# Second layer's attention run in steps between the eighths of the key, value and output products

## The reference, cut to what matters

```
kv = rms_norm(h, kv_norm_g) @ w_kv_b              # 1024 -> 2048
k1, k2, vb = split(kv)                            # 8 heads: 64, 64 and 128 wide
k1, k2 = rms_norm(k1, kn_b), rms_norm(k2, kn_b)
q1, q2 = rms_norm(split(rms_norm(h, ln_attn_g[1]) @ w_q), gq)
attn_map(q, k) = softmax(where(mask, q k^T * scale + bias))
a = attn_map(q1, k1) - lam * attn_map(q2, k2)
o = rms_norm(a @ vb, sub_g) * (1 - lam_init)
h = h + o @ w_o                                   # 1024 -> 1024
h = h + conv_ffn(rms_norm(h, ln_ffn_g[1]), ...)
```

## Time and profile before

| | us |
| --- | --- |
| median of three runs | 2471.53 |
| profiled execution, its own time | 2467.94 |
| its span, first to last instruction | 2466.6 |
| TensorE busy | 2309.0 (94%) |
| VectorE busy | 1464.0 (59%) |
| ScalarE busy | 933.3 (38%) |
| GpSimd busy | 454.1 (18%) |
| second layer's keys and values, 1676.6 to 1786.3 | 109.7 |
| its queries, to 1841.5 | 55.2 |
| its attention, 1847.1 to 2034.3 | 187.2 |
| its way out, to 2083.0 | 48.7 |

### The profile page before, as it was taken

How to read it: one execution, slowest core, us unless ns; L and a number is a source line. 1 busy time by engine, 2 the same in 40 slices (tenths; PEclk the granted TensorE clock), 3 DMA queues, 4 the chain that set the end, 5 groups by cost and what they waited for, 6 DMA issues and landing times.

```text
span 2466.6 us, 44116 instructions
## 1 busy us (share of the span) xinstructions
PE 2309.0 (94%) x19314; PEld 1995.0 (81%) x19314; DVE 1464.0 (59%) x2414; ACT 933.3 (38%) x1530; POOL 454.1 (18%) x245
## 2 busy tenths in 40 slices
PE   4998999999969999996999999999999999999999
PEld 1777777777757788774699999999986669999987
DVE  3678888888775533567637677333335544677632
ACT  1324443344332525233634344223345543444421
POOL 0344433433302435222220000000000002000000
PEclk7999999999989999897999999999995559999999
DMA  6531011111134234110022332333220002333332
GB/s 243 118 104 44 11 41 44 45 50 52 49 108 144 87 120 130 52 43 18 1 77 86 91 91 85 97 94 107 83 69 1 1 1 78 95 86 95 90 94 73
DMA packets 55680, 184.71 MB, mean 75 GB/s; under 512 B 6688, under 2 KB 6688, under 8 KB 55488
## 3 DMA queue, kind: packets, MB, share of 16 engines
q1 hardware_dynamic: 55488, 181.89, 24.2%
HBM read 174.99 MB, written 6.88 MB: 74 GB/s over the span
## 4 chain that ended last, share of the span: by engine, by line
PE 78%; DVE 13%; ACT 5%; issue 2%; DMA 1%; POOL 0%; SPq 0%; DVEq 0%; POOLq 0%; ACTq 0%
PE PS L518 60%; PE PS L648 4%; PE PS L981 3%; DVE ca L1695 3%; PE PS L949 3%; PE PS L964 1%; PE PS L843 1%; PE PS L904 1%; DVE Swk L2048 1%; DVE kx L1763 1%; DVE mx L2044 1%; ACT acc L1091 1%; ACT La L1091 1%; DVE Bf L1769 1%; PE PS L1062 1%
## 5 line engine op out<-in xcount | busy, mean ns | idle before, releaser
L2288 POOL TENSOR_TENSOR wlo<-raw,whi 128x1024 fp32r<-128x1024 f32 x122 | 301.3, 2471 | 979.8 <-ACT whi L1091 974.5
L518 PE MATMUL PS<-nhi,whi 128*128 128x264 f32 x2064 | 434.3, 292 | 2.4 <-DVE nlo L1936 2.4
L518 PE MATMUL PS<-nlo,whi 128*128 128x264 f32 x2064 | 422.7, 287 | 0.0
L518 PE MATMUL PS<-nhi,wlo 128*128 128x264 f32 x2064 | 420.6, 285 | 0.4 <-POOL wlo L2288 0.4
L1091 ACT ACTIVATE whi<-raw 128x1024 fp32r<-128x1024 f32 (+1 forms) x290 | 300.6, 1037 | 237.1 <-PE PS L518 209.0
L518 PEld LDWEIGHTS PS<-nhi,whi 128*128 128x128 f32 x2064 | 323.7, 191 | 18.0 <-issue 14.9
L518 PEld LDWEIGHTS PS<-nhi,wlo 128*128 128x128 f32 x2064 | 324.1, 191 | 0.6 <-POOL wlo L2288 0.6
L518 PEld LDWEIGHTS PS<-nlo,whi 128*128 128x128 f32 x2064 | 324.3, 190 | 0.0
L1607 DVE TENSOR_TENSOR wlo<-raw,whi 128x1024 fp32r<-128x1024 f32 (+1 forms) x168 | 201.2, 1198 | 187.5 <-ACT whi L1091 187.3
L518 PE MATMUL PS<-hhi,whi 128*128 128x512 f32 x648 | 264.2, 408 | 7.6 <-DVE hlo L1674 7.6
L518 PE MATMUL PS<-hhi,wlo 128*128 128x512 f32 x648 | 258.4, 399 | 1.5 <-POOL wlo L2288 1.5
(11 more groups left out here) (349 smaller groups left out, 3673.8 us busy)
## 6 DMA issues: line engine op xcount, KB each, us to landing
raw<-in_wall SPq DMA_DIRECT2D x298, 512.0 KB, 3.6
raw<-in_wall SPq DMA_DIRECT2D x16, 384.0 KB, 3.0
TZ<-g_rows SPq DMA_DIRECT2D x2, 2112.0 KB, 8.3
g_rows<-gsb SPq DMA_DIRECT2D x8, 328.0 KB
xt<-in_xT SPq DMA_DIRECT2D x1, 2048.0 KB, 13.1
o_rows<-os SPq DMA_DIRECT2D x8, 256.0 KB, 2.1
keep<-o_rows SPq DMA_DIRECT2D x8, 256.0 KB, 4.1
x<-in_xT SPq DMA_DIRECT2D x1, 2048.0 KB, 9.0
```

The lines of the kernel that those rows point to most:

```text
L518: q = e.matmul(out, cuts[a][:, k * P:(k + 1) * P], (hi_, lo_)[b][:, kr, lo:lo + w], start=start and k == 0 and a == b == 0, stop=stop and ...
L2288: e.tensor_tensor(wlo[slot[i]][:, w], raw[i % NRAW][:, w], whi[slot[i]][:, w].bitcast(F32), ALU.subtract).then_inc(*up("lo_pool", i))
```

## The change

The queries' units come first, with the rows scaled by ln_attn_g; then the operands are scaled anew by kv_norm_g. The key and value units are ordered by pairs of heads: key tiles p and 4 + p, value tiles 2p and 2p + 1. The way out is cut into 8 units of four blocks for heads 0 to 3 and 8 for heads 4 to 7, each added to H (steps res_b1 and res_b). Every program writes two lists of steps: "a" is one of four parts of an attention step, "g" one eighth of a product. A table sets their order on all engines: 32 g first (the first pair's keys and values), then for each of 8 heads the string BESIDE with 20 a and 16 g, then AFTER, whose g find nothing left. The g of heads 0 to 5 are the keys and values of the next pairs, those of heads 6 and 7 the first half of the way out.

The products keep banks 0 to 3. The attention has four: scores in 4 and 5 (one each, both for a 528 wide step), turned weights in 6, output and the turned remainder in 7. Both maps' maxima are negated in one instruction, both sums inverted in one, and ScalarE's exponentials wait for that one negation. Norms of keys use the product's own bank pair, as do the turned values; the head norm has a buffer of its own (sqb).

```diff
+BESIDE = "agagagagg" "agagagag" "agagagag" "aagaag" "aaaag"
+AFTER = "ag" * 10
...
-            for j in range(16):
-                units.append(("b_kv", j * P, 0, 8))
             for j in (0, 4, 1, 5, 2, 6, 3, 7):
                 units.append(("b_q", j * P, 0, 8))
-            for j in range(8):
-                units.append(("b_out", j * P, 0, 8))
+            for p in range(4):
+                for j in (p, 4 + p, 8 + 2 * p, 9 + 2 * p):
+                    units.append(("b_kv", j * P, 0, 8))
+            for k0 in (0, 4):
+                for j in range(8):
+                    units.append(("b_out", j * P, k0, 4))
...
+        def run_beside(attend, made):
+            for name in "g" * 32 + 8 * BESIDE + AFTER:
+                next(attend if name == "a" else made, None)
+            for part in (attend, made):
+                for _ in part:
+                    pass
...
-                    kr = order[k] if order else k0 + k
+                    kr = order[k0 + k] if order else k0 + k
...
-                normed("b_kv", ("kb_raw", k), (lambda k: on.wait_ge(*at("ffn0_n", k))) if k == 0 else None)
+                    normed("b_q", ("qb_raw", kt), (lambda k: on.wait_ge(*at("ffn0_n", k))) if (h, kt) == (0, 0) else None)
...
+            def made_beside():
+                def steps_of(what, b, hi_, lo_, rhs=None, order=None):
+                    for k, _ in enumerate(product(what, hi_, lo_, halves(T, b), rhs, order=order)):
+                        if k == 3 or (k == 1 and what == "b_out"):
+                            flush()
+                        yield
+                for p in range(4):
+                    for k in (p, 4 + p):
+                        b = banks["kb", k] = pair_of_banks(("kb_log", k))
+                        yield from steps_of("b_kv", b, nhi, nlo, (lambda k: on.wait_ge(*at("n2", k))) if k == 0 else None)
+                        def norm_k(k=k, b=b):
+                            on.wait_ge(*at("kb_sq", k))
+                            sums(sqh, T, b, blk).then_inc(*up("kb_sum", k))
+                        later.append(norm_k)
+                        yield
+                    for k in (2 * p, 2 * p + 1):
+                        b = banks["vb", k] = pair_of_banks(("Vb", k))
+                        yield from steps_of("b_kv", b, nhi, nlo)
+                        def turn_vb(k=k, b=b):
+                            on.wait_ge(*at("vb", k))
+                            turn_v(vTb[:, k % 2, :], b).then_inc(*up("vb_turned", k))
+                        later.append(turn_vb)
+                        yield
+                for j in range(8):
+                    b = pair_of_banks(("res_b1", j))
+                    yield from steps_of("b_out", b, ohi_b, olo_b, (lambda k: on.wait_ge(*at("ob", k))) if j == 0 else None, place)
+                    yield
...
+                def scores_free(bb, *then):
+                    for b in bb:
+                        for step in free_s[b]:
+                            on.wait_ge(*at(*step))
+                        free_s[b] = then
+                def scores(n, s):
+                    h, i = steps[n]
+                    q0, nq, w = rows_of(i)
+                    rows, kt = rowsof[h % 2], 4 * s + h // 2
+                    if n % 5 == 0:
+                        on.wait_ge(*at("qb", kt))
+                        on.wait_ge(*at("kb", kt))
+                    scores_free((4, 5) if w > 512 else (4 + s,), ("b_max", n, s))
+                    for out, lo, m_ in halves(w, 4 if w > 512 else 4 + s):
+                        q = e.matmul(out[0:nq, :], qB[rows, kt, q0:q0 + nq], kB[rows, kt, lo:lo + m_], start=True, stop=True)
+                    q.then_inc(*up("b_scores", n, s))
...
+                for n in range(N + 6):
+                    if n < N:
+                        scores(n, 0)
+                    yield
+                    if n < N:
+                        scores(n, 1)
+                    yield
+                    if 3 <= n <= N + 2:
+                        apply(n - 3)
+                    yield
+                    if 2 <= n <= N + 1:
+                        turn(n - 2)
+                    if n >= 8 and n % 5 == 3:
+                        h = n // 5 - 1
+                        on.wait_ge(*at("ob_sq", h))
+                        scores_free((4, 5), ("ob_log", h))
+                        sums(sqb, T, 4, ones).then_inc(*up("ob_sum", h))
+                    yield
...
+            run_beside(attend(), made_beside())
+            residual("b_out", "res_b", ohi_b, olo_b, "ob", order=place, first=4)
...
+            ffn(0, "ln_attn_g_2", 8)
...
+                def scores(n):
+                    h, i = steps[n]
+                    q0, nq, w = rows_of(i)
+                    on.wait_ge(*at("b_neg", n))
+                    for s in range(2):
+                        L = Lb[0:nq, 2 * (n % 3) + s, 0:w]
+                        act(L, L, ACT.Exp, bias=cell(n, s, 1), accum_out=cell(n, s, 2)).then_inc(*up("b_exp", n, s))
+                def weights(n):
+                    h, i = steps[n]
+                    q0, nq, w = rows_of(i)
+                    L = Lb[0:nq, 2 * (n % 3), 0:w]
+                    on.wait_ge(*at("b_inv", n))
+                    act(L, L, ACT.Copy, scale=cell(n, 0, 2)).then_inc(*up("b_scaled", n))
...
+                for n in range(N + 6):
+                    yield
+                    if n < N:
+                        scores(n)
+                    yield
+                    if 3 <= n <= N + 2:
+                        apply(n - 3)
+                    if 1 <= n <= N:
+                        weights(n - 1)
+                    yield
+                    if 2 <= n <= N + 1:
+                        turn(n - 2)
+                    if n >= 8 and n % 5 == 3:
+                        h = n // 5 - 1
+                        on.wait_ge(*at("ob_sum", h))
+                        power(sqb, T, 4, 1.0 / 128, 1e-6, ("ob_log", h), ("ob_rs", h))
...
+                for p in range(4):
+                    for k in (p, 4 + p):
+                        b = a_pair()
+                        yield from steps_of(8, 3)
+                        i = count.take()
+                        evac(kB[:, k, :], b, i, "kb_raw", k)
+                        def norm_k(k=k):
+                            on.wait_ge(*at("kb_rs", k))
+                            e.scalar_tensor_tensor(kB[:, k, :], kB[:, k, :], col("kn_b_2"), sqh[:, 0:T], ALU.mult,
+                                                   ALU.mult).then_inc(*up("kb", k))
+                        later.append(norm_k)
+                        ahead(i + 3)
+                        yield
...
+                def scores(n, s):
+                    h, i = steps[n]
+                    q0, nq, w = rows_of(i)
+                    L = Lb[0:nq, 2 * (n % 3) + s, 0:w]
+                    pv = PS[0:nq, 4 + s, 0:w] if w <= 512 else PS[0:nq, 4:6, 0:HT]
+                    on.wait_ge(*at("b_scores", n, s))
+                    if s == 0 and n >= 3:
+                        on.wait_ge(*at("b_turned", n - 3, 1))
+                    e.tensor_tensor_reduce(sv(L, w), pv, sv(tz(h, i), w), 1.0, LOW, ALU.add, ALU.max,
+                                           cells(n, 0)[:, s:s + 1]).then_inc(*up("b_max", n, s))
+                    if s:
+                        on.wait_ge(*at("b_max", n, 1))
+                        e.tensor_scalar(cells(n, 1), cells(n, 0), -1.0, None, ALU.mult).then_inc(*up("b_neg", n))
+                def weights(n):
+                    h, i = steps[n]
+                    q0, nq, w = rows_of(i)
+                    L, sums = [Lb[0:nq, 2 * (n % 3) + s, 0:w] for s in range(2)], cells(n, 2)
+                    on.wait_ge(*at("b_exp", n, 1))
+                    e.reciprocal(sums, sums).then_inc(*up("b_inv", n))
+                    on.wait_ge(*at("b_inv", n))
+                    e.tensor_tensor(sums[:, 1:2], sums[:, 1:2], lam[0:nq, 4:5], ALU.mult).then_inc(*up("b_lam", n))
+                    on.wait_ge(*at("b_lam", n))
+                    on.wait_ge(*at("b_scaled", n))
+                    e.scalar_tensor_tensor(L[0], L[1], sums[:, 1:2], L[0], ALU.mult, ALU.add).then_inc(*up("b_weights", n))
...
+                for n in range(N + 6):
+                    if n < N:
+                        scores(n, 0)
+                    yield
+                    if n < N:
+                        scores(n, 1)
+                    yield
+                    if 1 <= n <= N:
+                        weights(n - 1)
+                    yield
+                    if 2 <= n <= N + 1:
+                        turn(n - 2)
...
```

## The result

| | before | after |
| --- | --- | --- |
| median of four runs each, us | 2472.74 | 2428.87 |
| lowest to highest | 2460.05 to 2474.63 | 2428.07 to 2433.73 |
| ratio, with its 95% interval | | 0.9837 (0.9802 to 0.9873) |
| profiled execution, its own time | 2467.94 | 2428.51 |
| first product of the queries or keys to first product of the second FFN | 406.1 | 362.2 |

The kernel is 43.9 us faster. The forecast was 2412 us in a range of 2378 to 2448. The result lies in it, 16.9 us above the forecast.

The account below looks back on a forecast made before the run. The prediction took the second layer's attention to be bound by TensorE at half speed, with the VectorE-ScalarE chain second. Its terms summed to 349 us against 406, 57.5 less, giving 2412 us, with 8 in 10 for 2378 to 2448.

Parts of the forecast that it names:

- Point 1, queries: Query products, now first: 55.2 us as before plus about 1.4 for the half-speed start, 56.6 us.
- Points 2 and 3: Second scaling of the rows between products, 4.0 us with its 2.36 wait; then four units ahead of the heads, 25 us.
- Point 4, TensorE's side of the heads: TensorE's work in the eight heads: eighths 92, attention 95 at the upper clock, sums and turns 7; 194 us, 24.3 a head.
- Point 5, the loop: VectorE and ScalarE handing steps back and forth in the heads: 27.7 us a head for six, 25.7 for two; 224 with slack.
- TensorE sets the pace: Rival: one step's slack covers the loop of VectorE and ScalarE; heads 198 us, total 2386; chance 22%.
- the wait of the second 528 wide map: In the heads' 528 step, the second map's matmuls wait for the first map's maximum, sharing banks 4 and 5: 1.3 us.
- Point 6, the tail: Steps after the last product eighth with nothing beside them: about 7 us to the head sum and 6 from it, 13.
- Point 7, way out: Second half of the way out: 192 matmuls, 23.0 us, plus 2 for a half-speed start, 25; VectorE about 1 us behind.
- The rival of the low clock: Attention matmuls between products keep TensorE at 1.2 GHz in all heads: 388 us of work, stage about 373, total 2561; chance 6%.
- The signs: Interleaved stage: clock near 1.00, about 28 us a head, waits mostly on VectorE or ScalarE; wrong at 25 or less, over 31.
- the clock that doesn't rise: Rival: TensorE stays at 1.2 GHz in all heads despite the products beside them, total 2561; chance 6%.
- waits of the queues for each other: Rival: in-order queues in the heads stand at waits with needed work behind; 32 us a head, 256, total 2444; chance 22%.

Follow-up runs that it names:

- e8_tail: Changed kernel with the last 8 of the way out's first-half eighths moved from beside the last head to the tail: 2436.16 us, ratio 0.9864.
- the pairs: Changed kernel with a table that sets the eighths in pairs, as many per head: 2433.87 us, ratio 0.9850 to the kernel before.
- e5_whole_out: Changed kernel with the way out undivided after the attention, so the last two heads have no eighths beside them: 2451.93 us, ratio 0.9926.
- e6_n2_early: Changed kernel with the second scaling of the rows (n2) ahead of the norm of the last but one query: 2431.10 us, ratio 0.9848.
- fours: Changed kernel with eighths in fours in the three wide steps and pairs in the others: 2456.66 us, ratio 0.9932 to the kernel before.

## Why the prediction was near, and which step failed

- **The mechanism was right.** The attention ran at half speed, and eighths beside it bring the upper level: 0.99 in the heads, 0.55 with the same functions alone, 0.50 to 0.56 where only the last two heads lose their eighths.
- **What holds the level.** The kind of work matters, beyond the busy share: 20.00 of 20.00 us of attention alone were granted 0.50, 20.00 of 20.00 us of dense product 1.00. Attention alone did get the upper level at times, for some 8 us (from about 1887 to 1896), and lost it there without a wait right before; what raises it was not followed. The Trainium skill, TensorE: Matmul & The Clock Gate, "The HAM clock gate", names recent activity as what releases the throttle; by a plain reading a TensorE that never waits would be at the upper level. These traces do not agree: granted 0.50 from 1864 to 1884 us, and again for 15.00 of 15.00 us in e8_tail. "Part 4: PE-mode transpose" of the same page says that transposes do not count as busy in the same way. Turned weights are only 3.45 of the 23.75 us in the table of distances; so transposes alone would be a small part of it; which of the attention's matmuls matter was not separated.
- **Point 1, queries:** 55.6 us, forecast 56.6.
- **Points 2 and 3:** 33.8 us against 4.0 + 25. I took the wait of the earlier trace rows as it was, 2.36 us. There the scaling stood behind nothing; here ScalarE and VectorE have a query's norm and square ahead of it. The rule for a moved step is to name what is queued ahead of it, and I did not. It cost 2.7 us more of wait. The lower level behind it was in the forecast (1.6 us). Most of the rest is in the 32 eighths: by distances they took 26.06 us, 1.4 more than 23.0 and 1.6. Part of it is that the first two matmuls behind a norm sum take 0.43 us (1745.70 to 1746.13), not 0.24.
- **Point 4, TensorE's side of the heads: the step that failed.** I said 24.3 us a head on average. With key and value work the fifth head took 29.2. By the table of distances: 16 eighths 14.45 where I had 11.5 (0.90 each, not 0.72), and the attention with its head sum about 13.5 where I had 11.9. The 13.5 is 6.08 + 4.67 + 1.85 and about 0.97 for the sum, the distance of an unbroken one. The first is the price of each change between fp32 and fp32r matmuls, about 0.1 us into an eighth and 0.1 out of it towards scores; the pairs confirm it by taking 1.6 us of it away. The second is that halving the time of the lower level is too good by the part of each group that stays; and the 23.7 us that I halved were not all at the lower level (half of 0.7, so 0.3 of the 1.6).
- **Point 5, the loop: its pace was not the bound.** I had the loop at 27.7 and the heads at 224 us; they took 238.2 (1768.80 to 2007.00). Its own length behind TensorE was not measured, but taking much of it away gave 3.4 us. The rival "TensorE sets the pace" was right on who decides and wrong on the time, since it used the same 24.3. The forecast was near by luck: I took the wrong engine for the bound, and the length that I gave its loop happened to lie near what TensorE really needs. Single items came as said: the wait of the second 528 wide map is at most the 1.33 us of the fifth head (I had 1.3 for it).
- **One fall of the level** in the third head, to 0.90 in the mean, right after such a wait of 1.33 us, makes that head 3.3 us longer than the fourth or the sixth. It is no accident of one execution: the third head takes 33.4 to 33.5 us in e5_whole_out, e6_n2_early and e8_tail too, which have the same order up to there. The fifth head has the same wait with no fall; why only the third is not settled.
- **Point 6, the tail:** 8.6 us (2007.00 to 2015.6), forecast 13. The second half starts on its older heads' operands under the last head's exponent functions, with one wait of 0.85 us; I had let it wait for all four.
- **Point 7, way out:** 26.0 us, forecast 25 + 1.
- **The sum:** 55.6 + 33.8 + 238.2 + 8.6 + 26.0 = 362.2, where the forecast had 56.6 + 29 + 224 + 13 + 26 = 348.6. The differences are -1.0, +4.8, +14.2, -4.4 and 0: the heads are the miss.
- **Slips in the working.** A head without key and value work is put at 25.7 us, but 22.4 and four additions of 0.70 make 25.2; over two heads that is 1 us. The rival of the low clock has 388 us of TensorE work in a stage of 373; by its own 388 it would be 2576, not 2561. Neither bears on the result.
- **The signs.** The clock near 1.00 came, and so did the wait of the second 528 wide map. A head takes 29.8 us in the mean, nearer to the 31 where I would have called the forecast wrong than to the 28 that I expected, and the third takes 33.4. The chain of waits was to be on VectorE and ScalarE for the larger part, and it is on TensorE.

Of the rivals, the clock that doesn't rise did not happen; with no alternation the level stays low, but that kernel (2520.57 us) doesn't have the eighths at the lower level that the rival's 2561 counts. Long waits of the queues for each other are seen where eighths are bunched (fours, 2456.66 us).

## What to carry to other kernels

When two kinds of matmul are to be woven together, price the pieces as they will stand: a piece that takes 0.72 us in a row of its own kind took 0.90 alone between attention groups and 0.80 in pairs. Take the time of a group at the upper clock level from a row at that level, not from half of a row at the lower one. And before bunching pieces to save changes, ask which copy each piece covers: the waits for copies, and the falls of the clock right behind some of them, took back all that the pairs had saved.

## What the hardware showed that was not expected

- TensorE busy 20.00 of 20.00 us with attention alone was granted 0.50, and 27.9 of 28.2 us with 16 eighths beside the attention 1.00. With 8 eighths beside the last head, and behind a wait of 2.01 us, 15.00 of 15.00 us were granted 0.50. The busy share doesn't tell these apart.
- Every fall of the clock inside the heads of the changed kernel and of the pairs came right behind a wait of 1.20 to 2.56 us, though most waits had no fall behind them.
- A change from fp32 attention matmuls to the products' matmuls costs 0.34 us where two matmuls otherwise take 0.24, and the change back to scores the same again. Towards applied values of 128 rows it costs nothing (1893.89 to 1894.13, 0.24); towards those of 16 rows it does (1907.33 to 1907.67, 0.34).
- A wait removed at one place with the same queue order behind it came back 7 us later at 3.70 of its 5.08 us.
